# The opening of an encoder layer: x loaded by tile ahead of the constants, and the first query and key products started on four tiles

## The reference

```
h = rms_norm(x, pre_g)                       # per token: x * rsqrt(mean(x*x) + 1e-6) * gain
u = h @ w_in                                 # one projection, its columns split:
aq, ak, av, ag, bq, bk, bv, bg, cq, ck, cv, cg, mg = split(u)
lam = exp(sum(lp[0]*lp[1])) - exp(sum(lp[2]*lp[3])) + 0.2
ya = diff_attention(aq, ak, av, lam, subln_g, rel_bias) * silu(ag)   # T5 relative bias
yb = gqa_attention(...) * silu(bg)           # RMS-normalised, rotated q and k
yc = neighbourhood_attention(...) * silu(cg)
m = gates[0]*(ya @ wa) + gates[1]*(yb @ wb) + gates[2]*(yc @ wc)
x = x + rms_norm(m @ w_out, post_g)
x = x + sigmoid(x @ w_pg) * (p @ w_pe)
```

## Time and profile before

| | us |
|---|---|
| median of 3 runs (1394.3 to 1395.25) | 1395.13 |
| profiled execution | 1395.82 |
| its span, first to last instruction | 1394.0 |
| PE busy | 1346.5 (97%) |
| PE weight load busy | 1096.1 (79%) |
| VectorE busy | 573.2 (41%) |
| ScalarE busy | 525.0 (38%) |
| GpSimd busy | 295.7 (21%) |
| chain that ended last: PE's share | 91% |

### The profile page before, as it was taken

The page is one execution under the profiler, slowest core; times in us unless marked ns, Lnnn a source line. Parts: engine busy times, 40 slices in busy tenths (PEclk is TensorE's granted clock), DMA queues, the critical chain, the costliest instruction groups (busy, mean ns, idle before and its releaser), DMA issues.

```text
span 1394.0 us, 17290 instructions
## 1 busy us (share of the span) xinstructions
PE 1346.5 (97%) x6620; PEld 1096.1 (79%) x6620; DVE 573.2 (41%) x1111; ACT 525.0 (38%) x1002; POOL 295.7 (21%) x190
## 2 busy tenths in 40 slices
PE   4999999999999999999999999999998998999998
PEld 3778888788888767778888788888886887888887
DVE  5355545557100566675311224444434114335321
ACT  5355445553111466565311134444443113223210
POOL 1211222122222312130122313131211222213100
PEclk9999999999999999999999999999999999999999
DMA  5211111111111100000011210111100114322211
GB/s 187 78 39 39 39 39 49 54 32 49 46 46 45 59 18 16 16 16 24 31 46 53 75 46 31 61 31 61 31 24 23 53 46 145 127 68 83 69 38 38
DMA packets 25769, 72.09 MB, mean 52 GB/s; under 512 B 2872, under 2 KB 4792, under 8 KB 25568
## 3 DMA queue, kind: packets, MB, share of 16 engines
q1 hardware_dynamic: 25696, 71.09, 16.0%
HBM read 66.86 MB, written 4.23 MB: 51 GB/s over the span
## 4 chain that ended last, share of the span: by engine, by line
PE 91%; DVE 4%; ACT 2%; issue 1%; POOL 1%; DMA 0%; SPq 0%; ACTq 0%; DVEq 0%; POOLq 0%
PE ps L800 18%; PE ps L819 14%; PE ps L1155 12%; PE ps L1196 9%; PE ps L1335 6%; PE ps L1355 6%; PE ps L1044 5%; PE ps L1012 3%; PE ps L1125 2%; PE ps L981 2%; PE ps L842 2%; PE ps L957 2%; PE ps L897 2%; PE ps L1361 2%; PE ps L1076 1%
## 5 line engine op out<-in xcount | busy, mean ns | idle before, releaser
L629 POOL TENSOR_TENSOR w_lo<-stage,w_hi 128x1024 fp32r<-128x1024 f32 (+1 forms) x92 | 196.1, 2131 | 687.9 <-ACT w_hi L1405 687.9
L1405 ACT CAST w_hi<-stage 128x1024 fp32r<-128x1024 f32 (+1 forms) x92 | 86.2, 937 | 283.7 <-PE ps L800 199.0
L1893 DVE TENSOR_TENSOR pt_lo<-ps,pt_hi 128x512 fp32r<-128x512 f32 (+2 forms) x160 | 97.3, 608 | 131.6 <-ACT pt_hi L1533 71.3
L800 PE MATMUL ps<-h_hi,w_hi 128*128 128x512 f32 x368 | 114.1, 391 | 2.7 <-POOL w_lo L629 2.7
L800 PE MATMUL ps<-h_hi,w_lo 128*128 128x512 f32 x368 | 114.2, 392 | 0.0
L800 PE MATMUL ps<-h_lo,w_hi 128*128 128x512 f32 x368 | 113.8, 391 | 0.0
L819 PE MATMUL ps<-h_hi,w_hi 128*128 128x512 f32 x272 | 110.2, 405 | 0.0
L1155 PE MATMUL ps<-h_hi,w_hi 128*128 128x512 f32 x256 | 108.1, 422 | 0.0
L819 PE MATMUL ps<-h_hi,w_lo 128*128 128x512 f32 x272 | 106.3, 391 | 0.0
L819 PE MATMUL ps<-h_lo,w_hi 128*128 128x512 f32 x272 | 106.1, 390 | 0.0
L1155 PE MATMUL ps<-h_hi,w_lo 128*128 128x512 f32 x256 | 101.2, 395 | 0.0
(11 more groups left out here) (286 smaller groups left out, 2829.4 us busy)
## 6 DMA issues: line engine op xcount, KB each, us to landing
stage<-in_w_gates SPq DMA_DIRECT2D x24, 512.0 KB, 3.5
stage<-in_w_qkvg_a SPq DMA_DIRECT2D x19, 512.0 KB, 6.1
stage<-in_w_qkvg_c SPq DMA_DIRECT2D x16, 512.0 KB, 3.5
stage<-in_w_branch SPq DMA_DIRECT2D x24, 256.0 KB, 2.6
m<-in_x_tok SPq DMA_DIRECT2D x4, 1024.0 KB, 10.4
y<-in_x_tok SPq DMA_DIRECT2D x8, 512.0 KB, 3.6
stage<-in_w_pg SPq DMA_DIRECT2D x16, 256.0 KB, 3.1
out<-y SPq DMA_DIRECT2D x16, 256.0 KB, 2.0
```

Source lines behind the costliest of these rows:

```text
L629: nc.gpsimd.tensor_tensor(dst, stage[:, staged, 0:width], f32(hi), ALU.subtract).then_inc(w_ready, 1)
L800: done = mm(ps[:, bank + g, :], w[:, slot, k * P:(k + 1) * P], h[:, k, g * SEQ:(g + 1) * SEQ], start=first and part == 0, stop=last and pa ...
L1405: nc.scalar.copy(dst, stage[:, staged, 0:width]).then_inc(w_hi_done, 1)
L1893: sub = lambda out, whole, hi: nc.vector.tensor_tensor(out, whole, f32(hi), ALU.subtract)
```

## The change

x is loaded tile by tile, eight DMAs with a semaphore each, the first two ahead of every constant; the gain and the identity follow, then tiles 2 and 3, the T5 table, and the rest between the weights. The constants have semaphores of their own; lambda's rows are put into another buffer. The square is scaled by 1/1024 in ScalarE's own instruction, and GpSimd adds eps and takes the power, tile by tile; VectorE's step goes. PE transposes four tiles, then does the T5 product in banks 6 and 7, then the first group's queries and keys on those four tiles, with the transposes of tiles 4 to 7 in between. The keys are made by halves in banks 5 and 1, the queries in 4 and 0, each half with its own cast and subtraction. The lambda steps move behind the tiles on VectorE and ScalarE.

```diff
 # SyncE
-            (seven constants on const_in; x by two tiles, block 0 ahead of the last; block 1)
+            for t in range(2):
+                load_x(t)
+            sp.dma_start(vg[:, :], pre_g.broadcast_to([P, D])).then_inc(gain_in, 16)
+            sp.dma_start(ident[:, :], ident_in).then_inc(ident_loaded, 16)
+            for t in range(2, 4):
+                load_x(t)
+            sp.dma_start(tables[0:T5, 0:8], t5_table).then_inc(t5_in, 16)
+            sp.dma_start(y[0:T5, 1, :], t5_onehot).then_inc(t5_in, 16)
+            load_w(N_A, 0, w_qkvg_a[0])
+            for t in range(4, 6):
+                load_x(t)
+            load_w(N_A + 1, 1, w_qkvg_a[1])
+            for t in range(6, TILES):
+                load_x(t)
+            (subg, lambda_in, mask on const_in)
 # GpSimd
-                pool.wait_ge(x_var, LEAD + c + 1)
-                inv_sqrt(x_rstd[:, 2 * c:2 * c + 2], x_ss[:, 2 * c:2 * c + 2], x_pow)
+            def x_inv_sqrt(t):
+                pool.wait_ge(x_sq, LEAD + t + 1)
+                steps.done(pool, nc.gpsimd.tensor_scalar(x_ss[:, t:t + 1], x_ss[:, t:t + 1], EPS, None, ALU.add))
+                inv_sqrt(x_rstd[:, t:t + 1], x_ss[:, t:t + 1], x_pow)
+            for t in range(4):
+                x_inv_sqrt(t)
             split_w(N_A, 0)
+            for t in range(4, 6):
+                x_inv_sqrt(t)
             split_w(N_A + 1, 1)
+            for t in range(6, TILES):
+                x_inv_sqrt(t)
             spread_bias(0)
 # TensorE
+            FIRST_BANKS = {("q", 0): 4, ("k", 0): 5, ("q", 1): 0, ("k", 1): 1}
+            def turn_x(t):
+                pe.wait_ge(x_scaled, LEAD + t + 1)
+                if t >= 3:
+                    pe.wait_ge(h_ready, LEAD + t - 2)
+                if t == 4:
+                    pe.wait_ge(f_saved, LEAD + 1)
+                turn(x_row(t), X_BANKS[t % 3], x_turned)
+            pe.wait_ge(ident_loaded, 16)
+            for t in range(4):
+                turn_x(t)
+            pe.wait_ge(t5_in, 32)
+            pe.wait_ge(h_ready, LEAD + 2)
             for c in range(2):
-                done = mm(ps[0:8, c, :], tables[0:T5, 0:8], y[0:T5, 1, c * 512:(c + 1) * 512],
+                done = mm(ps[0:8, X_BANKS[1] + c, :], tables[0:T5, 0:8], y[0:T5, 1, c * 512:(c + 1) * 512],
                           start=True, stop=True)
             done.then_inc(f_turned, 1)
+            first_product("q", 0, range(2))     # waits for its weight block and for 4 tiles of h_lo
+            turn_x(4)
+            first_product("q", 0, range(2, 5))
+            turn_x(5)
+            first_product("q", 0, range(5, KC))
+            turn_x(6)
+            first_product("k", 0, range(4))
+            turn_x(7)
+            first_product("k", 0, range(4, KC))
+            first_product("q", 1, range(KC))    # waits for 8 tiles of h_lo
+            first_product("k", 1, range(KC))
             half_step(-2, lambda T: None)
 # ScalarE
+            for t in range(4):
+                square_x(t)
+            h_hi_part(0)
+            h_hi_part(1)
+            split_w(0, 0, 1)
+            h_hi_part(2)
+            square_x(4)
+            h_hi_part(3)
+            square_x(5)
+            split_w(N_A + 1, 1, 1)
+            square_x(6)
+            act.wait_ge(f_turned, LEAD + 1)
+            nc.scalar.copy(y[0:8, 0, :], ps[0:8, X_BANKS[1]:X_BANKS[1] + 2, :].rearrange("p b n -> p (b n)")) \
+                .then_inc(f_saved, 1)
+            square_x(7)
+            for t in range(4, TILES):
+                h_hi_part(t)
+                if t == 6:
+                    first_hi("q", 0)
+            (lambda's exp)
+            first_hi("k", 0)
+            first_hi("q", 1)
             split_a(N_A + 2)
+            first_hi("k", 1)
             split_a(N_A + 3)
 # VectorE
+            dve.wait_ge(gain_in, 16)
+            for t in range(3):
+                h_scale(t)
+            h_lo_part(0)
+            h_scale(3)
+            for t in range(1, 4):
+                h_lo_part(t)
+            for t in range(4, 7):
+                h_scale(t)
+            h_lo_part(4)
+            h_scale(7)
+            for t in range(5, TILES):
+                h_lo_part(t)
+            first_lo("q", 0)
+            (lambda's steps, ones2, subg; wait for the stored T5 bias; ones_sq)
+            first_lo("k", 0)
+            first_lo("q", 1)
+            first_lo("k", 1)
             max_a(0)
```

More of the change, by code:

```diff
@@ L211, in build_program @@
         const_in = sem("const_in")
-        x_in = [sem(f"x_in{i}") for i in range(4)]
+        gain_in = sem("pre_gain_in")
+        ident_loaded = sem("ident_in")
+        t5_in = sem("t5_table_in")
+        first_half = sem("first_halves_done")
+        x_in = [sem(f"x_in{i}") for i in range(TILES)]
         lam_summed = sem("lambda_summed")
@@ L789, in _ @@
             last = UNITS - 1
-            for signal in (f_turned, x_turned, half_done, va_turned, rope_turned, bh_done, mixed_first, b_turned, b_back, scores, p_turned, p0_turned, mixed,
+            for signal in (f_turned, x_turned, first_half, half_done, va_turned, rope_turned, bh_done, mixed_first, b_turned, b_back, scores, p_turned, p0_turned, mixed,
                            ss_done, spread, r_done, x2_turned, pe_done):
@@ L1632, in merge, with h_hi_part @@
                 merge_tanh(b, 7, n + 13, 1)
[L1635 to L1638, removed]
             def square_x(t):
-                act.wait_ge(x_in[t // 2], 16)
+                act.wait_ge(x_in[t], 16)
                 act.wait_ge(x_sq, LEAD + t - 1)
[L1642 to L1651, removed]
+                nc.scalar.activation(y[:, 2 + t % 2, :], x_row(t), ACT.Square, scale=D ** -0.5,
+                                     accum_out=x_ss[:, t:t + 1]).then_inc(x_sq, 1)
+            def h_hi_part(t):
                 act.wait_ge(x_turned, LEAD + t + 1)
@@ L1896, in _ @@
                 dve.sem_inc(signal, LEAD + UNITS)
-            for signal in (lam_summed, x_var, x_scaled, h_ready, out_w_split, first_ready,
+            for signal in (lam_summed, x_scaled, h_ready, out_w_split, first_ready,
                            qa_ready, ka_ready, va_ready, ga_ready,
@@ L2090, in merge, with h_scale, h_lo_part, first_lo @@
                 merge_add(b, 7, n + 15, 1)
-            dve.wait_ge(const_in, 16 * 7)
+            def h_scale(t):
+                dve.wait_ge(x_pow, LEAD + t + 1)
+                stt(out=x_row(t), in0=x_row(t), scalar=x_rstd[:, t:t + 1], in1=vg[:, :], op0=ALU.mult,
+                    op1=ALU.mult).then_inc(x_scaled, 1)
+            def h_lo_part(t):
+                dve.wait_ge(h_hi_done, LEAD + t + 1)
+                sub(h_lo[:, :, t * P:(t + 1) * P], banks(X_BANKS[t % 3]).rearrange("p (k q) -> p k q", k=KC),
+                    h_hi[:, :, t * P:(t + 1) * P]).then_inc(h_ready, 1)
+            def first_lo(name, g):
+                src, cols = ps[:, FIRST_BANKS[name, g], :], slice(g * SEQ, (g + 1) * SEQ)
+                if name == "q":
+                    dve.wait_ge(qa_hi_done, LEAD + g + 1)
+                    stt(out=q_lo[:, cols], in0=src, scalar=SCALE, in1=f32(q_hi[:, cols]), op0=ALU.mult,
+                        op1=ALU.subtract).then_inc(qa_ready, 1)
+                else:
+                    dve.wait_ge(ka_hi_done, LEAD + g + 1)
+                    sub(k_lo[:, cols], src, k_hi[:, cols]).then_inc(ka_ready, 1)
+            dve.wait_ge(gain_in, 16)
[12 more added lines that the diff above has]
+            first_lo("q", 0)
+            dve.wait_ge(const_in, 16 * 3)
             steps.done(dve, nc.vector.memset(ones2, 1.0))
@@ L2102, in _ @@
             steps.done(dve, nc.vector.tensor_scalar(lam, lam, LAMBDA_INIT, None, ALU.add))
[L2104 to L2125, removed]
             dve.wait_ge(f_stored, 16)
```

64 lines of the change are left out of this document (17 added, 47 removed).

## The result

The changed kernel takes 1383.08 us (median of 4 runs, 1381.55 to 1383.46) against 1395.19 for the kernel before beside it: a ratio of 0.9908, 95% interval 0.9891 to 0.9925. The forecast was 1383.0. The profiled execution took 1383.11 with a span of 1381.2. PE is busy for 1343.4 us (97%), VectorE 574.4, ScalarE 525.3, GpSimd 303.5.

What follows compares the result with a forecast made beforehand. PE, busy 97%, bounds the kernel, so the opening counts: its end moves from 57.5 to 45.2, taking 12.3 us off 1395.82 to 1383.5, and 0.7 lower for the median, 1383. Range 1381 to 1385; with rivals 1 to 3, 1380.5 to 1387.5.

Steps and rivals of the forecast that it cites:

- rival 4: After the opening: a later PE wait keeps its place and the gain is given back, 1395 us; chance 0.03.
- Tile 3 lands at 9.9: Loads of x: tile 3 lands at 9.5 to 10.3 us by transfer rate, middle 9.9.
- ScalarE is the chain to the saved bias, 11.35 us: Opening: ScalarE's squares, casts and copy from tile 3 take 11.35 us, ending at 21.3; tile 4's transposes wait for it.
- T5 costs nothing: T5 product behind four tiles: ends by 19.3 to 19.9 at half clock, before ScalarE reaches the copy at 20.3.
- 90 products and four sets of transposes, 23.9: PE after 21.3: 20.4 us of products plus 3.5 of transposes, so the opening ends at 45.2.
- The clock from the T5 product on: PE in the opening: granted clock 1.00 from 20 us on, products at 0.227 us each.
- Rival 1: PE in the opening: half clock until the products, price 2.1 us, 1385.1 us; chance 0.16.
- Full speed during transposes: PE's early transposes: earlier trace's first 24 ran near half speed, the next eight at full, so PE came up during transposes.
- A clock dip may come or go, 1 to 2 us: After the opening: where PE waits, a clock dip may come or go with the shift, 1 to 2 us.
- rival 2: GpSimd's first power in the opening: not ready when asked, 1384.4 us, or 1390 if only at 14.5; chance 0.09.
- rival 3: End of the opening: store takes 9.1 us again, weight 2 late, PE waits 2.4 to 3.5, 1386.5 us; chance 0.06.
- rival 5: PE at half clock through the opening, 25.7 us more, 1408.7 us; a loss once some 56 products run slowly; chance 0.04.

Runs made afterwards that it cites:

- e4: The changed kernel profiled once more with no edit: 1382.60 us, opening ended at 45.64.
- e6: Against the changed kernel, ScalarE saves the T5 bias two instructions earlier and GpSimd makes tile 6's factor ahead of weight 1's split: 1383.67 us.
- e2: Against the changed kernel, the order of the products undone, loads kept: 1387.77 us.
- e12: The kernel of e6 (T5 bias saved earlier, no products of ones) run again unchanged: 1381.78 us.
- e8: The changed kernel timed again with no edit: 1382.82 us.
- long fill: Changed kernel plus products of ones on idle PE, 18 before tile 0's transposes: 1385.99 us; with T5 bias also saved earlier 1382.63 and 1382.75.
- short fill: Changed kernel plus products of ones on PE, only 8 before tile 0's transposes, and the T5 bias saved earlier: 1382.92 us.
- e3: The kernel before the change profiled once more with no edit: 1393.96 us.

## Why the prediction was right, point by point

**The opening moves one block.** Right. The waits of PE behind 64 us are those of before (6.7, five times, 2.4), so nothing was given back (rival 4).

**Tile 3 lands at 9.9.** Its square started at 10.55, so 0.65 late and beyond the 10.3 of the slow end; tile 2's began at 9.02. In windows of half a microsecond the DMAs moved 404 GB/s up to 10.0, then 246 and 205, then 385: the stretch in which tile 3 ends and the one-hot matrix, 32 partitions wide and next on the queue, comes in. Whether the one slows the other was not shown; a sum by a mean rate has no room for it.

**ScalarE is the chain to the saved bias, 11.35 us.** 10.55 to 21.39 is 10.84, 0.5 shorter: each instruction starts about 0.1 before the one ahead of it ends, which outweighs the four reads of the sums behind the squares (0.19 each) that the prediction left out. This error and the late tile cancel, by luck, and 21.39 stands against 21.3. That this chain is the bound holds at full clock (e4 waits 1.0 for it, e6 frees it). In the profiled execution it was not: PE itself got to tile 4 only at 21.78.

**T5 costs nothing.** Right: it ended at 18.5, before ScalarE came to the copy at 20.40. In e2, at half clock, it took 3.57 from 16.90, and still only the copy was waited for.

**90 products and four sets of transposes, 23.9.** Right in e4: 45.64 - 21.43 = 24.2. In the profiled execution 25.47: 9 products at 2.66 instead of 2.07 and 8 transposes at 1.71 instead of 0.87 make up the 1.5.

**The clock from the T5 product on: the step that failed.** The forecast had granted clock 1.00 from 20 on. Rival 1 had nearly the size (2.1; measured 1.5 to 1.6 between e4 and the two others, 1.7 between e6 and e12) but not the course: PE was not slow until the products, it had come up (tile 3's transposes at 1.10) and fell again at 17.9. Of five executions without fill, the change itself or with the early copy, three fell (after, e8, e12) and two did not (e4, e6). Three with a long fill did not fall, one with a short fill did. What decides it stays open; of the three that held at a long fill the rows show that PE worked without a gap from 4.99 until behind the T5 product.

**Full speed during transposes.** For slow ones has 1.71 us for eight, 0.214 each, where the earlier trace rows has the granted clock at 0.50. The kernel after shows again that PE came up during transposes, now without the T5 product ahead: it had done nothing but transposes when tile 3's eight ran in 1.10 us, against 1.91 for tile 4's eight at a granted clock of 0.50. The granted clock reads 1.00 in every window up to 16, also where the first 24 run slowly (5.69 us in all; those of 10 to 12 take about 0.18 each), so this rests on the durations.

**The rest of the run: mis-sized.** "A clock dip may come or go, 1 to 2 us" was the allowance; 2.5 came. Two windows of the kernel after, and the two of before at the same work (10 us later):

```profile
550.00:555.00 5.00, 5.00 (x24) 3.63 (x21) 1.86 (x4) 1.31 (x2) 0.00 (x0) 0.66 0.00 0
...
1045.00:1050.00 5.00, 3.22 (x17) 2.62 (x18) 1.54 (x3) 1.40 (x4) 1.28 (x1) 1.00 0.20 52
```
```profile
560.00:565.00 5.00, 5.00 (x25) 3.73 (x22) 1.07 (x4) 0.85 (x2) 0.00 (x0) 0.69 0.00 0
...
1055.00:1060.00 5.00, 3.14 (x12) 2.23 (x11) 1.64 (x4) 2.54 (x8) 1.28 (x1) 0.80 0.02 2
```

The stretch near 550 came both times, the one near 1045 only before; so did one near 790. The table shows the trend: 6.8 us of half clock goes with a rest of 1333.5 to 1334.0, 17 with 1336.1 to 1338.1. It is not exact: a stretch that falls where PE idles costs less, as in e3, where 6.9 of the 13.7 came at 1180 to 1187 while PE waited for part of the time. The falls differ between executions of one program (e4 and e8), and the kernel before itself had a rest of 1336.5 and one of 1334.8, so this gain of 2.5 is not shown to be the change's. With e4's opening and the first rest of before, the profiled execution would have taken 45.64 + 1336.5 + 1.8 = 1383.9, where the forecast's own sum for it was 1383.5; with e3's rest, 1382.2.

**GpSimd ready (rival 2).** Refuted. Its timeline:

```profile
5.72 0.22 POOL L632 TENSOR_SCALAR small<-small 128x1 f32<-128x1 f32 x1 [3.94 <-ACT y L1666]
6.02 0.57 POOL L625 TENSOR_TENSOR small<-small 128x1 f32<-128x1 f32 x1
```

The first added EPS began right behind its square and took 0.22 (0.3 taken; up to 1.32 later, hidden). The first power followed at 6.02 and took 0.57.

**Weight 2 (rival 3).** Refuted. The store was confirmed after 1.4 (2 taken, 9.1 feared); the cast at 42.34 waited for PE, not for the load, and GpSimd's split ended 1.4 before PE wanted it (1.0 by the forecast, whose 44.2 includes the cast of 1.05, though its sum does not name it):

```profile
SPq L527 <- DMA f_scratch<-y: 1.4, 1, 1.4
```
```profile
43.46 2.40 POOL L644 TENSOR_TENSOR w_lo<-stage,w_hi 128x1024 fp32r<-128x1024 f32 x1 [7.75 <-ACT w_hi L1433]
```

**Slower (rival 5).** Refuted: about 9 of the 96 products ran at half clock (six, and 0.59 / 0.22 of the next nine), not 56.

## What to carry to other kernels

Where one engine is busy for 97% and nothing behind the opening waits on it, an opening is worth what it shortens, one for one: here 4.4 to 4.8 us from loading the data ahead of the constants that are needed later, and 2.6 to 3.2 from giving PE work on the tiles already there. Count the chain of the engine that feeds the bound, instruction by instruction; its length came out within 0.5 us of 10.84, and its end within 0.1 only because the start was off the other way. And before a gain of one or two microseconds is put down to an edit, run the unchanged kernel twice: here its opening alone was 45.6 or 47.2, and the untouched rest 1333.7 or 1335.0.

## What the runs showed of the hardware

- The granted clock fell from 1.00 to 0.50 while PE was at work, not only behind an idle stretch such as the 3.3 us of the earlier trace rows (0.59 in 27 to 28 us of before): in e12 amid six products in a row (the third took 0.40 us, the fourth 0.45, the fifth 0.63), in the kernel after within the T5 product (1.00 in 17.0 to 17.5, 0.79 in 17.5 to 18.0). One program showed it in one execution and not in the next (after and e8 fell, e4 did not).
- Some instructions of VectorE and GpSimd took longer side by side. In the kernel after a scaling of 128x1024 takes 1.28 us mostly and took 3.40 where it began beside a weight split on GpSimd; it ended 1.1 after that split. GpSimd's add on 128x1 ranges from 0.22 to 1.32 and its power from 0.57 to 1.44, the long ones beside a scaling. That the other engine is the cause was not tested, and the scaling from 13.77 took 1.28 with a split of 2.75 beside it from 14.54. VectorE and GpSimd in the kernel after:

```profile
20.39 3.40 DVE L2134 SCALAR_TENSOR_TENSOR m<-m,small,vg 128x1024 f32<-128x1024 f32 x1 [0.47 <-POOL small L625]
```
```profile
20.33 2.38 POOL L644 TENSOR_TENSOR w_lo<-stage,w_hi 128x1024 fp32r<-128x1024 f32 x1
```

- A store of 32 KB was confirmed in 1.4 us in the kernel after, issued at 21.41 with a DMA share of 0.00 from 20 to 22, against 9.1 in the kernel before, issued at 11.90 with a DMA share of 1.04 in 14 to 16.
